# Condition's row ahead of the experts' rows, and the DRAM scratch zeroed in the second feed-forward unit

## The reference, cut to what matters

```python
mod = c_act @ w_ada[l] + b_ada[l]                   # c_act = silu(c)
...
h2 = modulate(rmsnorm_2(x, g_ffn[l]), sh2, sc2)
pg_top, g_idx = lax.top_k(pg, 1)                    # 1 of 4 groups
pe_top, e_idx = lax.top_k(pe, TOP_K)                # 2 of the group's 8 experts
...
for e in range(N_EXPERTS):                          # 32
    he = jax.nn.silu(t @ w1e[e]) * (t @ w3e[e])     # 1024 -> 256
    out = out + cw[:, e:e + 1] * (he @ w2e[e])      # 256 -> 1024
```

## Time and profile before

| | |
|---|---|
| time, median of 3 runs | 1598.81 us (1598.29 to 1599.84) |
| profiled execution | span 1595.2 us; its own time with what lies around the span is not recorded, the median run is 3.6 us longer |
| TensorE busy | 1534.1 us (96%) |
| VectorE / ScalarE / GpSimd busy | 1056.8 / 748.6 / 48.0 us |
| SP's queue (q1) | 344.92 MB, 54.5% of 16 engines over the span |
| GpSimd's queue (q0) | 9.11 MB, 1.6% |
| read from / written to DRAM | 365.64 / 12.06 MB |

### The profile page before, as it was taken

One profiled execution on the slowest core, in us unless ns is written; L12 is line 12 of the kernel. 1 busy time (PEld: TensorE's weight loads), 2 busy tenths in 40 slices (PEclk: granted clock), 3 DMA queues, 4 the chain that ended last, 5 costly groups with the idle time before them and its releaser, 6 DMA issues.

```text
span 1595.2 us, 29188 instructions
## 1 busy us (share of the span) xinstructions
PE 1534.1 (96%) x12098; PEld 1324.8 (83%) x12098; DVE 1056.8 (66%) x2091; ACT 748.6 (47%) x1552; POOL 48.0 (3%) x62
## 2 busy tenths in 40 slices
PE   7999999999999999999989999999999999998997
PEld 7999987889999999998879999999979894332234
DVE  7677775787877787778787787777797546221123
ACT  7455465565544554546365544464743233221124
POOL 0000001000000000000000000000000000222100
PEclk9999999999999999999999999999999998999998
DMA  9746643044666457655314556634410197999994
GB/s 346 292 164 260 263 185 132 1 185 160 251 256 271 170 215 278 250 218 238 126 55 189 238 222 272 256 130 172 151 51 3 51 367 303 408 416 418 418 421 168
DMA packets 55140, 357.75 MB, mean 224 GB/s; under 512 B 9653, under 2 KB 9909, under 8 KB 13152
## 3 DMA queue, kind: packets, MB, share of 16 engines
q1 hardware_dynamic: 48960, 344.92, 54.5%
q0 software_dynamic: 5472, 9.11, 1.6%
q10 hardware_dynamic: 576, 1.86, 0.3%
HBM read 365.64 MB, written 12.06 MB: 237 GB/s over the span
## 4 chain that ended last, share of the span: by engine, by line
PE 81%; DMA 8%; DVE 6%; ACT 3%; issue 1%; SPq 0%; ACTq 0%; DVEq 0%; POOLq 0%
PE ps L433 21%; PE ps L435 21%; PE ps L434 21%; PE ps L2943 5%; DMA AR<-in_w 4%; PE ps L2977 2%; DMA ring<-in_w 2%; DMA AR<-slot_rows 1%; PE ps L2115 1%; PE ps L1186 1%; ACT SQ L1120 1%; DVE WL L420 1%; PE ps L2687 1%; DVE HL L638 1%; PE ps L1098 1%
## 5 line engine op out<-in xcount | busy, mean ns | idle before, releaser
L433 PE MATMUL ps<-HH,WH 128*128 128x256 f32 x1696 | 480.2, 283 | 16.6 <-DVE WL L420 11.7
L420 DVE TENSOR_TENSOR WL<-ring,WH 128x512 fp32r<-128x512 f32 x728 | 450.6, 684 | 46.2 <-ACT WH L409 38.5
L434 PE MATMUL ps<-HL,WH 128*128 128x256 f32 x1696 | 477.9, 282 | 0.0
L435 PE MATMUL ps<-HH,WL 128*128 128x256 f32 x1696 | 477.9, 282 | 0.0
L409 ACT ACTIVATE WH<-ring 128x512 fp32r<-128x512 f32 x728 | 395.5, 622 | 82.1 <-PE ps L435 65.8
L433 PEld LDWEIGHTS ps<-HH,WH 128*128 128x128 f32 x1696 | 320.0, 189 | 19.5 <-DVE HL L638 14.7
L434 PEld LDWEIGHTS ps<-HL,WH 128*128 128x128 f32 x1696 | 320.0, 189 | 0.1
L435 PEld LDWEIGHTS ps<-HH,WL 128*128 128x128 f32 x1696 | 320.0, 189 | 0.0
L433 PE MATMUL ps<-AH,WH 128*128 128x256 f32 x704 | 198.4, 282 | 0.2 <-DVE AL L810 0.2
L434 PE MATMUL ps<-AL,WH 128*128 128x256 f32 x704 | 198.1, 281 | 0.0
L435 PE MATMUL ps<-AH,WL 128*128 128x256 f32 x704 | 198.1, 281 | 0.0
(11 more groups left out here) (575 smaller groups left out, 2217.4 us busy)
## 6 DMA issues: line engine op xcount, KB each, us to landing
ring<-in_w SPq DMA_DIRECT2D x246, 1024.0 KB, 6.9
AR<-in_w SPq DMA_DIRECT2D x67, 1024.0 KB, 21.5
SQ<-in_w SPq DMA_DIRECT2D x5, 1024.0 KB
cols<-in_s SPq DMA_DIRECT2D x1, 2994.0 KB
SQ<-in_w SPq DMA_DIRECT2D x4, 512.0 KB, 6.6
slot_rows<-RG SPq DMA_DIRECT2D x1, 2048.0 KB, 21.2
AR<-slot_rows SPq DMA_DIRECT2D x2, 1024.0 KB, 19.0
cons<-in_k ACTq DMA_DIRECT2D x1, 1634.0 KB
```

Of the source, the lines that this page charges most:

```text
L420: ins = v.tensor_tensor(lo(n)[:, s], ring[:, i % RING, s], hi(n)[:, s].bitcast(F32), ALU.subtract)
L433: pe.matmul(out, ah, bh, start=start, stop=False, skip_group_check=skip)
L434: pe.matmul(out, ah, bl, start=False, stop=False, skip_group_check=skip)
L435: return pe.matmul(out, al, bh, start=False, stop=stop, skip_group_check=skip)
```

## The change

1. `weight_rows` puts `("c", 0)` between the stages' rows and the experts' rows. It is now row 222; the experts' rows follow from 223 on; there are still 319. `sync_row` finds the row by name.
2. `zeros` is now 128 columns of a constant (`madd1`), which are zero in every partition, loaded at the start of the program. GpSimd's memset is gone; `pool_tables` waits for `d_zero` in its place, and the later counts of `g_mr` are one lower.
3. The DMA that zeroes Z moves from `sync_experts` to SP's ring loop, right behind the load of the row `("f2_0d", 4)` (step 4 of the second feed-forward unit). It writes 32 pieces of 128 floats a partition where it wrote 8 of 512. It waits for the constants.
4. `d_zero` is a semaphore of its own. VectorE's and ScalarE's waits for it in the experts' part are gone; GpSimd's first scatter still has one.

```diff
-    return slot_order() + [("moe" + x, e) for e in range(N_EXP) for x in "abd"] + [("c", 0)]
+    return slot_order() + [("c", 0)] + [("moe" + x, e) for e in range(N_EXP) for x in "abd"]
...
-        d_zero, d_back = d_ring[2], d_ring[3]
+        d_back = d_ring[3]
+        (d_zero,) = signals("d_zero")
...
-        zeros = S12
+        zeros = KC("madd1", 0, 128)
...
             q.wait_ge(p_raw, 8)
-            pool.memset(zeros, 0.0).then_inc(*q.up(g_mr))
+            q.wait_ge(d_zero, 16)
             pool.iota(slot1, [[1, 512]], base=1, channel_multiplier=0, allow_small_or_imprecise_dtypes=True)
...
-            q.wait_ge(g_mr, 2)
+            q.wait_ge(g_mr, 1)
...
             v.tensor_scalar(ELf, ELf, -200.0, None, ALU.max).then_inc(*q.up(v_mr))
-            q.wait_ge(d_zero, zeroed + 16)
             v.tensor_tensor(SD, ident.unsqueeze(1)...
...
-            q.wait_ge(g_mr, 3)
+            q.wait_ge(g_mr, 2)
...
                 if i == 0:
-                    q.wait_ge(d_zero, zeroed + 16)
                     for n, x in enumerate((S12, C12)):
...
-                if m == 4:
-                    q.wait_ge(g_mr, 1)
-                    sp_.dma_start(Z.rearrange("(p a) (b d) -> p (a b) d", p=P, b=2), zeros.unsqueeze(1).broadcast_to([P, 8, 512])).then_inc(d_zero, 16)
...
-                        q.wait_ge(d_zero, zeroed + 16)
+                        q.wait_ge(d_zero, 16)
                     pool.indirect_dma_start(Z, ...
...
                     sync_row(sp_, q, order[n - RING][0][:-1])
+                if order[n] == ("f2_0d", 4):
+                    q.wait_ge(d_cons, 16)
+                    sp_.dma_start(Z.rearrange("(p a) (b d) -> p (a b) d", p=P, b=8), zeros.unsqueeze(1).broadcast_to([P, 32, 128])).then_inc(d_zero, 16)
```

More of the change, by code:

```diff
@@ L2581, in build @@
         loads = expert_loads()
-        zeroed, back = [16 * sum(1 for s in range(len(order)) if s % RING == b) for b in (2, 3)]
+        back = 16 * sum(1 for s in range(len(order)) if s % RING == 3)
         wout_ring = [split_slots[at[("wout2", g)]] for g in range(4)]
```

## The result

| | before | changed |
|---|---|---|
| time, median of 5 runs | 1598.29 us (1596.94 to 1599.84) | 1584.95 us (1583.12 to 1587.04) |
| ratio, 95% interval | | 0.9919 [0.9907, 0.9931] |
| span of the profiled execution | 1595.2 us | 1581.3 us |

13.3 us less; 1583.9 us had been forecast, 14.9 less than a before of 1598.8. The page of the changed kernel: GpSimd's queue moves 1.77 MB where it moved 9.11, and the zeroing lands 14.6 us after its issue.

The account below looks back on a forecast made before the run. The experts' weight stream at 418 GB/s and the read-back set the end, TensorE close behind. Span 1595.2 - 14.9 (12.5 + 2.4) + 0 for zeroing = 1580.3, plus 3.6 around it: 1583.9 us; range 1580 to 1590.

Parts of the forecast that it names:

- seven idle places: Rounds 16 to 19: seven places without an expert each load 1 MB nobody needs; the change drops 7.34 MB.
- Five tiles in the full stream: Experts, useless tiles issued at 1395, 1439 and 1491: 2.51 us each at 418 GB/s, 12.5 us saved.
- The first pair: Experts, first two useless tiles, 1352 to 1363: a hole in the stream leaves 2.4 of their 5.0 us as gain.
- TensorE's limit: Experts: TensorE could give back at most 18.2 us from late weights and the read-back.
- Zeroing at the experts' start: Start of the experts: removing the memset, the 2 MB DMA and two waits gains zero.
- Zeroing in the feed-forward unit: Second feed-forward unit: 2 MB in 512-byte pieces takes 9 us, 5.0 free; just hidden, 0 cost, at most 15.0 us.
- The upper end of 95 ns: Feed-forward zeroing: a 512-byte piece might cost what a 2 KB one did, 95 ns, taking 24.2 us.
- (a): Rival, experts' stream: saved bytes become more holes; second pair too gives only 2.4 us, gain 12.3, 1586.5 us; chance 0.17.
- (b): Rival, experts: TensorE becomes the bound and loses nothing more, gain 18.2 us, 1580.6 us; chance 0.09.
- (c): Rival, feed-forward unit: zeroing at 60 to 70 ns a piece stalls 6 to 9 us, 1590 to 1593 us; chance 0.08.
- (d): Rival, feed-forward unit: pieces over 95 ns make it slower; at 120 ns TensorE stalls 21.5 us, 1605 us; chance 0.03.
- (e): Rival, experts: the idle rounds still load, if the expert number weren't 32; chance 0.01.

Follow-up runs that it names:

- the order without a hole: Changed kernel with the first further round two places later, the second one: 1580.67 us; with the condition's row back behind the experts' rows, 1598.83 us.
- the first pair loaded: Changed kernel with the old order of rows, but only the first idle round's two 1 MB tiles loaded: 1588.66 us, ratio to before 0.9933.
- the row alone: Kernel before with only the condition's row moved, zeroing left at the start of the experts' loads: 1584.80 us, ratio to before 0.9914.
- The kernel that zeroes twice: Changed kernel with a second DMA of the same size and shape, into another DRAM tensor, in front of the zeroing: 1589.70 us, ratio to before 0.9933.
- the half tiles: Changed kernel with SP loading only the first half of each weight tile from the fourth round of the order on: 1581.69 us, ratio to before 0.9883.
- the zeroing alone: Changed kernel with the condition's row back behind the experts' rows, so only the zeroing has moved: 1599.29 us, ratio to before 0.9998.

## Why the prediction was right

The chain of causes held at each link: seven idle places, 7.34 MB (7.34 measured), a full stream, a hole behind the third round, an end set by the stream and the read-back. The read-back landed at 1558.1 where 1558 had been named, but 1.7 us of that came from the earlier first turn. The terms by size:

- Five tiles in the full stream, 12.5 us: no run took these five alone. The changed kernel's 13.4 less the 1.2 of the first pair leave 12.2 us for them. The tiles of the order without a hole cost 16.9 / 7 = 2.4 us each.
- The first pair, 2.4 us: measured 1.2. The step that was off is the count of bytes delivered up to 1363: I took the stream as full from 1359 on and 1.0 MB ahead by 1363. It restarted below that rate (335 GB/s from 1357 to 1361), and 16 us behind the first turn the changed kernel was 0.75 MB ahead; 20 to 29 us later 0.5 to 0.6 MB of them were left. No gap ate the rest: over those 20 us the engines were as busy as before and moved 412 GB/s where they had moved 420 (the changed kernel first, then the kernel before). Three more executions with the hole show 407 to 411 there, two more with the first pair loaded 418 and 423; why the stream is slower behind a hole, no run shows. The whole, 14.9 forecast and 13.4 measured, is off by this term for the most part.

```profile
1361.12:1381.12 20.00, 20.00 (x96) 6.62 (x94) 4.80 (x13) 4.87 (x9) 4.21 (x4) 1.00 1.01 412
1362.81:1382.81 20.00, 20.00 (x96) 6.62 (x94) 4.80 (x13) 4.87 (x9) 4.04 (x4) 1.00 1.02 420
```

- TensorE's limit, 18.2 us: 18.7.
- Zeroing at the experts' start, nothing: the row alone, with the zeroing in its old place, has the same time within the noise.
- Zeroing in the feed-forward unit, nothing on TensorE: right, with more room than I gave it. I had 34 to 36 ns a piece, 9 us, and loads 4 us late. The split for the third load came 1.5 us late (434.65 against 432.73, less the 0.45 by which TensorE's release is later in this execution), so with the 5.0 us that were free the zeroing took some 6.5 us, an estimate: 25 ns a piece. The kernel that zeroes twice shows the same price directly (last section). VectorE's low part ended at 443.16, 2.8 us before TensorE's release of VectorE at 445.93, where 0.2 us had been left over. The upper end of 95 ns, on which the rivals of no change and of slower rested, was far off.
- The waits for weights, under 3 us: 2.0 us remained, and 2.5 us for the read-back.

The span came out 1.0 us above the forecast 1580.3 rather than 1.5 because the clock's spells ahead of and behind the rounds fell differently (1.7 us gained, 1.2 lost in the profiled execution). The median, too, is 1 us above its forecast, where the gain was 1.6 us short (13.3 for 14.9): the kernel before came out 0.5 us lower than the 1598.8 that I had started from. Nor do 3.6 us lie around the span, as the sum has it: the profiled execution of the changed kernel took 1583.1 for its span of 1581.3, so 1.8 us lie there, and the other 1.8 are its distance from the median. The sum came out because the profiled execution of the kernel before lay about as far under its own median. How the clock's spells fall is chance: the second profile of the changed kernel has its first turn at 1350.41, 5.3 us later than the first.

Of the rivals, (a) had the right direction, since the gain fell short of the forecast, and the wrong place: going by the 12.2 us above, which are a remainder, the second pair was worth its bytes. (b) is excluded by the half tiles, (c) and (d) by the zeroing alone, (e) by the bytes of the queue.

## What to carry to other kernels

A gather that "loads nothing" for an unused place does so only if its index is out of bounds for every part; what it hits instead costs its bytes in a full stream (here 2.3 to 2.5 us a MB). Price removed bytes by where they ran: seven equal tiles were worth 13.4 us in an order that leaves a hole and 16.9 us in one that doesn't, and closing the hole afterwards gave another 4 to 5 us for a change of one tuple. An extra transfer fits between two bursts of a paced queue without cost until the wait behind it reaches the bound engine. Here it then cost more than the wait, 7.2 us for 3.8, since the clock dropped as well.

## What the runs showed of the hardware

In the kernel that zeroes twice, the 12 us from 420 to 432 hold almost nothing but pieces of 512 bytes written to DRAM: 7637 - 16 = 7621 of 7639 packets. They went at 327 GB/s, a fifth under the 418 of the weights, which is 16 x 12 us / 7621 = 25 ns a piece and engine. The 2 KB pieces of the earlier trace rows, mixed with weights, went at 342. I had expected a larger loss, 34 to 36 ns a piece.

```profile
DMA packets 7639, 3.93 MB, mean 327 GB/s; under 512 B 16, under 2 KB 7637, under 8 KB 7637
```

"DMA: Bandwidth & Descriptors" of the Trainium skill (Specifications) puts the line rate at 512 bytes and up; by these rows it is not reached.

TensorE's clock cost nearly as much as the waits: behind waits of 2.0 and 1.8 us its mean granted clock was 0.57 for 4 us each, most of it at the lower of its two levels (1.2 GHz of 2.4), and 3.8 us of waiting became 7.2 us of delay.
